# Feed-forward rows in tiles of 512 columns, and every product operand at 0 modulo 256 bytes

## The chip, the cores and the metric

The kernel runs on one core of one Trainium2 chip, as one launch. The metric is the device time of that launch in microseconds. Three runs before the change took 887.83 us in the median, from 887.15 to 888.42.

## The reference

The reference is one block of a hybrid network on 16 learned rows followed by 512 input rows, each of 1024 numbers in fp32:

```python
u = rms_norm(h, norm_mix_pre) @ w_in            # 528 x 1024 @ 1024 x (3*512 + 1792 + 2*1024)
u_sb, u_rw, gate_sb, gate_rw = split(u)
o_sb = stick_breaking_attention(*split(u_sb))   # 8 heads of 64
o_rw = rwkv7_time_mix(token_shift(u_rw), ...)   # 8 heads of 64, a recurrence over the rows
merged = sigmoid(gate_sb) * (o_sb @ w_branch_sb) + sigmoid(gate_rw) * (o_rw @ w_branch_rw)
h = h + rms_norm(merged @ w_out, norm_mix_post)
f = rms_norm(h, norm_ffn_pre)
f = (silu(f @ w_ffn_gate) * (f @ w_ffn_up)) @ w_ffn_down   # inner width 2816
h = h + rms_norm(f, norm_ffn_post)
return h[:, 16:]
```

## The kernel before

Activations lie transposed: features on the 128 partitions, rows of the sequence along the free axis. A matrix product is made on TensorE in the type fp32r, and for precision each operand is kept as a rounded half (`_hi`) and the rest (`_lo`). Three products stand for one: hi by hi, hi by lo, lo by hi. So each tile of 128 input features (`k`, eight of them for a width of 1024) costs three matmuls for each 128 output features, each matmul with its own weight load before it.

A weight tile is called a unit: 128 by 1024 numbers, 512 KB. SP loads it into one of four buffers `w_raw`, ScalarE rounds it to `w_hi` (two buffers), VectorE subtracts to `w_lo` (two buffers), and TensorE then makes 24 matmuls of it in `products` (L578 to L589). The units come in a fixed order, and semaphores count them: `w_split` after the subtraction, `w_used` after the last matmul.

The stages, in the order of time, and which operand streams through the array (moving) and which is loaded into it (stationary):

- The input projection (L586, in `products`) and ten of its gate units, which are cut in two halves and put between the steps of the mixing (L1672). Moving: `h_hi`, `h_lo`, the normed rows, 528 columns wide for each `k`. Stationary: `w_hi`, `w_lo`.
- The mixing of the heads, about 184 to 396 us: small fp32 matmuls of 64 by 64 (L1616), attention products (L1783 to L1847), and running sums with a triangle (L1818, L1824, L1828), where `softplus_hi` and `softplus_lo` are moving and `tri_r` is stationary. Each engine follows an order that is written out by hand.
- The branch products (L586 again, with `osb_hi`, `osb_lo`, `orw_hi`, `orw_lo` as the moving operand), with the same loop and the same order hi-hi, hi-lo, lo-hi.
- The output projection, in blocks of 128 rows (L1893, `block_products`): here the weights `wo_hi`, `wo_lo` (and `w_hi`, `w_lo`) are moving, in halves of 512 columns, and `merged_hi`, `merged_lo` are stationary. After each block VectorE and ScalarE norm the rows, TensorE transposes them (L1498), ScalarE copies the transposed block from PSUM into `h_hi` (L799, called by `out_hi`) and VectorE writes the rest into `h_lo` (L1112, called by `out_lo`). These are the feed-forward rows: 512 of them, written over the rows of the input projection, which is done by then.
- The first two feed-forward units (L1936) on the first 384 columns, with the last block's transposition between them, then on the last 128 columns.
- The other 42 feed-forward units (L586), a loop of four units a turn, moving `h_hi` and `h_lo`, 512 columns.
- The down projection (L1893): moving `w_hi`, `w_lo`, `wd_hi`, `wd_lo`, stationary `act_hi`, `act_lo`; and the last norm, of which little is left after the last product.

All of SBUF is laid out by hand with a running cursor (`sb`, L257), from the first byte that is free, 16,481 in this build, rounded up to 32: 16,512, which is 128 modulo 256. `h_hi` and `h_lo` are declared as [128, 8, 528] of four bytes, so that one `k` follows the other at 2,112 bytes, eight times 256 and 64. The weight buffers step by 512 bytes a `k`; `osb`, `orw`, `merged`, `act` by 2,048. The vector `p_chunk` (144 bytes) leaves the cursor 32 bytes off, so that `bonus` and all that lies behind it stand at 96 modulo 256.

Of the kernel before, what the change touches and what calls it, by code (L numbers as in the profile page):

```python
# [28 lines left out]
F32 = mybir.dt.float32  # L29
F32R = mybir.dt.float32r  # L30
# [4 lines left out]
P = 128  # L35
D = 1024
SEQ = 512
META = 16
T = META + SEQ
HALF = T // 2  # L40
KT = D // P
# [29 lines left out]

RAW = 4
SPL = 2

BLOCKS = (4, 0, 1, 2, 3)

# [52 lines left out]
OUT_ORDER = (0, 1, 2, 3)  # L129
FIRST = 3 * P  # L130
WO_FIRST = 2
OUT_BANKS = (6, 0, 2, 4)
# [114 lines left out]
def build(nc, x, meta, w_in, w_sb, w_rw, w_out, w_g, w_u, w_d, decay_up, aaa_up, gate_up,  # L247
          vecs, g_mix_pre, g_mix_post, g_ffn_pre, g_ffn_post, kf, kb, out):
    with ExitStack() as ctx:
# [5 lines left out]
        cursor = [base]  # L255

        def sb(name, shape, dt=F32):  # L257

            size = 1
            for n in shape[1:]:  # L260
                size *= n
            size *= 1 if dt == U8 else 4
            t = nc.alloc_sbuf_tensor_at(name, shape, dt, offset=cursor[0])
            cursor[0] += (size + 31) // 32 * 32
            assert cursor[0] <= end, (name, cursor[0], end)
            return t


        raw = [sb(f"w_raw{i}", [P, 1024]) for i in range(RAW)]
        w_hi, w_lo = [], []  # L270
        for i in range(SPL):
# [22 lines left out]
        h_hi = sb("h_hi", [P, KT, T], F32R)  # L294
        h_lo = sb("h_lo", [P, KT, T], F32R)
        ffn_at = cursor[0]
        cursor[0] = ffn_at - 2 * KT * T * 4
        held_hi = [sb(f"wd_hi{i}", [P, 1024], F32R) for i in range(HELD - SPL)]
        held_lo = [sb(f"wd_lo{i}", [P, 1024], F32R) for i in range(HELD - SPL)]
# [4 lines left out]
        kv_at = cursor[0]  # L304
# [9 lines left out]
        vv = sb("v_t", [P, PAIRS, TP])  # L314
        sg = sb("sig_xg", [P, T])
        pc = sb("p_chunk", [P, PAIRS, NC_])
        bonus_at = cursor[0]
        bonus = sb("bonus", [P, PAIRS, SEQ])
        mix_at = cursor[0]
# [111 lines left out]
        def bank(b, n=512):  # L431
            return psum[:, b, 0:n]
# [15 lines left out]
        def quads(b, n):  # L448

            return psum[:, b, 0:PAIRS * n].rearrange("p (q n) -> p q n", q=PAIRS)  # L450
# [12 lines left out]
        w_used = sem("w_used")  # L463
# [6 lines left out]
        n_lo = sem("norm_lo")  # L470
# [107 lines left out]
        def products(u, w0, outs, xh, xl, kts, last=False):  # L578

            hi, lo = w_hi[u % SPL], w_lo[u % SPL]  # L580
            n = 0
            total = 3 * len(kts)
            for i, k in enumerate(kts):
                for w, xs in ((hi, xh), (hi, xl), (lo, xh)):
                    for o, (c0, c1) in outs:
                        mm = nc.tensor.matmul(o, w[:, (w0 + i) * P:(w0 + i + 1) * P], xs[:, k, c0:c1],  # L586
                                              start=(n == 0), stop=(n == total - 1))
                    n += 1
            return mm  # L589
# [201 lines left out]
        def _(act):  # L791
            s_ = nc.scalar

            def norm_hi(n, width, c0, b=None):

                b = 4 + n % 4 if b is None else b
                for h in range(2):
                    act.wait_ge(n_tp, n + h + 1)
                    s_.activation(h_hi[:, 4 * h:4 * h + 4, c0:c0 + width], quads(b + h, width),  # L799
                                  ACT.Copy).then_inc(n_hi, 1)  # L800


# [109 lines left out]
            for kind, n, s in ORDER_ACT:  # L912
# [10 lines left out]
                if kind == "seq":  # L923
                    if s in ("bh", "kh"):
                        act.wait_ge(mix_pe, last_of(MIX_PE, "seq", c, ("T0", "T1", "T2")))
                        dst, c0 = {"bh": (bh, 0), "kh": (kh, 128)}[s]
# [22 lines left out]
                if kind == "sum":  # L949
# [9 lines left out]
                    if s == "w1":  # L959
                        act.wait_ge(mix_dve, last_of(MIX_DVE, "sum", h, ("s2", "s3")))  # L960
                        w = z_h[:, PART[1]]
                        s_.activation(w, w, ACT.Exp).then_inc(mix_act, 1)
                    if s == "w0":
                        act.wait_ge(mix_dve, last_of(MIX_DVE, "sum", h, ("s0", "s1")))
                        w = z_h[:, PART[0]]
                        s_.activation(w, w, ACT.Exp).then_inc(mix_act, 1)
                if kind == "att":
# [5 lines left out]
                    if s == "wm":  # L973
                        for h in (2 * n, 2 * n + 1):
                            act.wait_ge(mix_dve, upto(MIX_DVE, "sum", h, "s4"))
                        w = zm[n // 2][64 * (n % 2):64 * (n % 2) + 64, :]
# [6 lines left out]
            for kind, i in LATE:  # L983
# [20 lines left out]
                if kind == "unit":  # L1004
                    u = U_MIX + EARLY + i
# [52 lines left out]
                tail_root(b, TAIL_1_ACT.index(f"sq_f{n}") + 1)  # L1058

            def out_hi(n):  # L1060
                norm_hi(10 + 2 * n, P, P * OUT_ORDER[n], OUT_BANKS[OUT_ORDER[n]])

            out_square(0)
            out_square(1)
# [40 lines left out]
        def _(dve):  # L1105
            v_ = nc.vector

            def norm_lo(n, width, c0, b=None):
                b = 4 + n % 4 if b is None else b
                for h in range(2):  # L1110
                    dve.wait_ge(n_hi, n + h + 1)
                    v_.tensor_sub(h_lo[:, 4 * h:4 * h + 4, c0:c0 + width], quads(b + h, width),  # L1112
                                  h_hi[:, 4 * h:4 * h + 4, c0:c0 + width].bitcast(F32)).then_inc(n_lo, 1)

            def mean(i):

# [304 lines left out]
                v_.tensor_scalar(ztok[b][:], ztok[b][:], small[:, 24 + b:25 + b], None, ALU.mult).then_inc(tail_dve, 1)  # L1421

            def out_lo(n):
                norm_lo(10 + 2 * n, P, P * OUT_ORDER[n], OUT_BANKS[OUT_ORDER[n]])

            dve.wait_ge(rows_in, 48)
            out_gain(0)
# [60 lines left out]
        def _(pe):  # L1488
# [442 lines left out]
            def ffn_part(s, ks, c0, c1):  # L1931

                hi, lo = split(U_FFN + s)
                for k in ks:
                    for i, (w, xs) in enumerate(((hi, h_hi), (hi, h_lo), (lo, h_hi))):
                        mm = t_.matmul(psum[:, s, c0:c1], w[:, k * P:k * P + P], xs[:, k, c0:c1],  # L1936
                                       start=(k == 0 and i == 0), stop=(k == KT - 1 and i == 2))
                return mm
# [11 lines left out]
            def ffn_unit(i, s):  # L1950

                per = 2 * len(TAIL_FFN)
                ahead, t = s // RAW, s % RAW // 2
                u = U_FFN + s
                pe.wait_ge(w_split, i * RAW + (u + 1))
                step = 1 + s % 2
                pe.wait_ge(tail_dve, i * per + (FFN_AT + ahead * per + (t - 2) * len(TAIL_FFN) + step))
                products(u, 0, [(bank(s % RAW), (0, SEQ))], h_hi, h_lo, range(KT)).then_inc(w_used, 1)

            with pe.Fori(0, N_FFN_LOOP - 1) as i:  # L1960
                for s in range(2, RAW + 2):
# [72 lines left out]
```

## Time and profile before

| | |
|---|---|
| median of three runs | 887.83 us |
| span of the profiled execution | 883.6 us |
| left around the span | 4.2 us |
| TensorE | 98% of the span, 8165 matmuls |
| weight loads | 81%, beside the matmuls |
| VectorE, ScalarE, GpSimd | 55%, 47%, 11% |
| DMA | 82.82 MB, mean 94 GB/s |

The profiled execution's own time on the metric's clock is not given; the page has its span, from the first to the last instruction, and 4.2 us is the difference of that span to the median of the other three. A matmul's duration in the profile is modelled and longer than the time it holds the array, since the next one starts before the last has ended: the time that one costs is read from start to start.

### The profile page before, as it was taken

The numbers are of one execution on the slowest core, as the hardware profiler recorded it, in microseconds if no ns is written. First come the engines' busy times: TensorE is split into PE (matmuls) and PEld (weight loads), VectorE is DVE, ScalarE is ACT, GpSimd is POOL, SyncE is SP. The second block draws the span as 40 slices with busy tenths as digits, with TensorE's granted clock in tenths as the row PEclk, the third lists the DMA queues.
The fourth block names the chain that finished last, engine by engine and source line by source line (L and its number), as shares of the span: only waits on it lengthen the run. The fifth ranks groups of instructions, "written<-read, shape, count | busy, mean of one in ns | idle before, by whom it ended". The sixth has DMA issues, their size and how long they took to land.

```text
span 883.6 us, 18916 instructions
## 1 busy us (share of the span) xinstructions
PE 868.9 (98%) x8165; PEld 717.8 (81%) x8165; DVE 486.9 (55%) x642; ACT 411.2 (47%) x572; POOL 94.8 (11%) x92
## 2 busy tenths in 40 slices
PE   6999999999999999999999999999999999999997
PEld 5999999877877788668888898888888888888886
DVE  6459997245865767439575854444444444322333
ACT  6445566269777787464353532222222222211331
POOL 2015544111010111052000000000000000000000
PEclk9999999999999999999999999999999999999999
DMA  9332213321210011222369123333333333223321
GB/s 281 99 96 73 87 57 96 125 63 55 68 45 22 22 39 56 76 77 72 123 210 294 49 85 94 93 93 92 94 92 93 91 94 96 94 97 103 102 77 72
DMA packets 109584, 82.82 MB, mean 94 GB/s; under 512 B 3471, under 2 KB 100025, under 8 KB 109258
## 3 DMA queue, kind: packets, MB, share of 16 engines
q1 hardware_dynamic: 109514, 81.77, 30.4%
q8 instruction: 58, 0.95, 0.4%
q14 instruction: 12, 0.10, 0.0%
HBM read 75.99 MB, written 5.77 MB: 93 GB/s over the span
## 4 chain that ended last, share of the span: by engine, by line
PE 93%; DVE 4%; issue 1%; ACT 1%; DMA 0%; DVEq 0%; SPq 0%
PE psum L586 47%; PE psum L1893 19%; PE psum L1616 8%; PE psum L1672 7%; PE psum L1818 2%; PE psum L1936 2%; PE psum L1507 1%; PE psum L1828 1%; PE psum L1799 1%; DVE w_lo L576 1%; PE psum L1847 1%; DVE shift_diff L1178 1%; PE psum L1498 1%; DVE k_mod L1219 1%; DVE v_t L1183 1%
## 5 line engine op out<-in xcount | busy, mean ns | idle before, releaser
L586 PE MATMUL psum<-h_hi,w_hi 128*128 128x512 f32 (+2 forms) x736 | 230.2, 348 | 0.8 <-DVE w_lo L576 0.8
L586 PE MATMUL psum<-h_lo,w_hi 128*128 128x512 f32 (+2 forms) x736 | 229.4, 347 | 0.0
L586 PE MATMUL psum<-h_hi,w_lo 128*128 128x512 f32 (+2 forms) x736 | 228.5, 346 | 0.0
L576 DVE TENSOR_TENSOR w_lo<-w_raw,w_hi 128x1024 fp32r<-128x1024 f32 x69 | 88.8, 1288 | 120.9 <-ACT w_hi L571 116.5
L586 PEld LDWEIGHTS psum<-h_hi,w_hi 128*128 128x128 f32 x736 | 127.8, 188 | 22.3 <-issue 1.9
L586 PEld LDWEIGHTS psum<-h_lo,w_hi 128*128 128x128 f32 x736 | 127.5, 188 | 18.4 <-issue 0.5
L586 PEld LDWEIGHTS psum<-h_hi,w_lo 128*128 128x128 f32 x736 | 128.0, 188 | 17.8
L1090 ACT ACTIVATE w_hi<-w_raw 128x1024 fp32r<-128x1024 f32 x44 | 46.7, 1061 | 171.7 <-PE psum L586 164.4
L1453 DVE TENSOR_TENSOR w_lo<-w_raw,w_hi 128x1024 fp32r<-128x1024 f32 x44 | 53.9, 1225 | 130.6 <-ACT w_hi L1090 126.5
L571 ACT ACTIVATE w_hi<-w_raw 128x1024 fp32r<-128x1024 f32 x70 | 73.7, 1055 | 74.4 <-PE psum L1893 56.2
L1893 PE MATMUL psum<-w_hi,act_hi 128*128 128x512 f32 x144 | 45.7, 390 | 0.0
L1893 PE MATMUL psum<-w_hi,act_lo 128*128 128x512 f32 x144 | 45.7, 389 | 0.0
L1893 PE MATMUL psum<-w_lo,act_hi 128*128 128x512 f32 x144 | 45.7, 389 | 0.0
L1672 PE MATMUL psum<-h_hi,w_hi 128*128 128x512 f32 x80 | 32.7, 408 | 0.0
L1672 PE MATMUL psum<-h_lo,w_hi 128*128 128x512 f32 x80 | 31.7, 396 | 0.0
L1893 PEld LDWEIGHTS psum<-w_hi,act_hi 128*128 128x128 f32 x144 | 26.9, 188 | 5.8 <-DVE w_lo L576 0.2
L1893 PEld LDWEIGHTS psum<-w_hi,act_lo 128*128 128x128 f32 x144 | 27.0, 188 | 5.7
L1893 PEld LDWEIGHTS psum<-w_lo,act_hi 128*128 128x128 f32 x144 | 27.0, 188 | 5.6
L1672 PE MATMUL psum<-h_hi,w_lo 128*128 128x512 f32 x80 | 31.4, 393 | 0.0
L857 ACT ACTIVATE shift_in<-psum 128x528 f32<-128x528 f32 x14 | 8.6, 613 | 33.5 <-PE psum L586 29.8
L1336 DVE TENSOR_TENSOR scores<-scores,psum 128x128 f32<-128x128 f32 (+3 forms) x32 | 15.4, 482 | 13.1 <-PE psum L1828 12.7
L958 ACT ACT_TABLE_LOAD x16 | 20.5, 1283 | 0.3
(306 smaller groups left out, 1522.9 us busy)
## 6 DMA issues: line engine op xcount, KB each, us to landing
w_raw<-in_w_in SPq DMA_DIRECT2D x30, 512.0 KB, 3.8
w_raw<-in_w_g SPq DMA_DIRECT2D x22, 512.0 KB, 3.7
w_raw<-in_w_u SPq DMA_DIRECT2D x22, 512.0 KB, 3.8
w_raw<-in_w_d SPq DMA_DIRECT2D x22, 512.0 KB, 3.5
w_raw<-in_w_in SPq DMA_DIRECT2D x48, 128.0 KB, 2.2
w_raw<-in_w_out SPq DMA_DIRECT2D x8, 512.0 KB, 5.4
kept_gates<-gate_raw SPq DMA_DIRECT2D x10, 256.0 KB, 2.1
sig_t<-kept_gates SPq DMA_DIRECT2D x10, 256.0 KB, 2.8
```

Source lines behind the costliest of these rows:

```text
L571: nc.scalar.activation(split(u)[0][:], raw[u % RAW][:], ACT.Copy).then_inc(w_hi_done, 1)
L576: nc.vector.tensor_sub(lo[:], raw[u % RAW][:], hi[:].bitcast(F32)).then_inc(w_split, 1)
L586: mm = nc.tensor.matmul(o, w[:, (w0 + i) * P:(w0 + i + 1) * P], xs[:, k, c0:c1], start=(n == 0), stop=(n == total - 1))
L958: s_.activation(part, part, ACT.Ln, bias=1.0).then_inc(mix_act, 1)
L1090: s_.activation(w_hi[v % SPL][:], raw[v % RAW][:], ACT.Copy).then_inc(w_hi_done, 1)
L1336: v_.tensor_tensor(d, d, psum[:, CBANK, SEQ - WIDTH[j]:SEQ], ALU.subtract).then_inc(mix_dve, 1)
L1453: v_.tensor_sub(w_lo[v % SPL][:], raw[v % RAW][:], w_hi[v % SPL][:].bitcast(F32)).then_inc(w_split, 1)
L1616: mm = t_.matmul(psum[rows(p, hd, moved), bnk + p // 2, o0:o0 + n], w(k, p), m(k, p), start=first, stop=last, skip_group_check=True)
L1672: mm = t_.matmul(bank(GBANK), w[:, k * P:(k + 1) * P], xs[:, k, META:T], start=(k == 0 and i == 0), stop=(k == KT - 1 and i == 2))
L1818: t_.matmul(psum[:, CBANK, SEQ - WIDTH[i]:SEQ], tri_r[:, P:2 * P], part[:, OFF[i]:OFF[i] + WIDTH[i]], start=False, stop=False, skip_group_ ...
L1893: mm = t_.matmul(bank((2 * b if at is None else at) + h), xs[:, k, P * b:P * b + P], w[:, 512 * h:512 * h + 512], start=(k == 0 and i == 0 ...
L1936: mm = t_.matmul(psum[:, s, c0:c1], w[:, k * P:k * P + P], xs[:, k, c0:c1], start=(k == 0 and i == 0), stop=(k == KT - 1 and i == 2))
```

## The change

Five things are done.

1. Before the first buffer the cursor is rounded up to 256, so that memory begins at 16,640 and not at 16,512. Everything up to `p_chunk` moves by 128 bytes.
2. Before `bonus` the cursor is rounded up to the same place modulo 256 as `kT`, which moves `bonus` and all behind it by 160 bytes in all.
3. Two new tensors, `f_hi` and `f_lo`, are [128, 8, 512], one `k` every 2,048 bytes. They begin where `h_hi` and `h_lo` begin.
4. ScalarE and VectorE write the feed-forward rows into them.
5. All feed-forward products read them.

No instruction is added, removed or moved, and no wait is changed. `h_hi` and `h_lo` keep their 528 columns for the input projection and the gates.

```diff
+LINE = 256
@@ layout
+        cursor[0] += -cursor[0] % LINE
         raw = [sb(f"w_raw{i}", [P, 1024]) for i in range(RAW)]
...
         ffn_at = cursor[0]
+        f_hi, f_lo = (nc.alloc_sbuf_tensor_at(n, [P, KT, SEQ], F32R, offset=ffn_at - i * KT * T * 4)
+                      for n, i in (("f_hi", 2), ("f_lo", 1)))
...
         pc = sb("p_chunk", [P, PAIRS, NC_])
+        cursor[0] += (kv_at - cursor[0]) % LINE
         bonus_at = cursor[0]
@@ ScalarE
-            def norm_hi(n, width, c0, b=None):
+            def norm_hi(n, width, c0, b=None, hi=h_hi):
...
-                    s_.activation(h_hi[:, 4 * h:4 * h + 4, c0:c0 + width], quads(b + h, width),
+                    s_.activation(hi[:, 4 * h:4 * h + 4, c0:c0 + width], quads(b + h, width),
...
             def out_hi(n):
-                norm_hi(10 + 2 * n, P, P * OUT_ORDER[n], OUT_BANKS[OUT_ORDER[n]])
+                norm_hi(10 + 2 * n, P, P * OUT_ORDER[n], OUT_BANKS[OUT_ORDER[n]], f_hi)
@@ VectorE
-                    v_.tensor_sub(h_lo[:, 4 * h:4 * h + 4, c0:c0 + width], quads(b + h, width),
-                                  h_hi[:, 4 * h:4 * h + 4, c0:c0 + width].bitcast(F32)).then_inc(n_lo, 1)
+                    v_.tensor_sub(lo[:, 4 * h:4 * h + 4, c0:c0 + width], quads(b + h, width),
+                                  hi[:, 4 * h:4 * h + 4, c0:c0 + width].bitcast(F32)).then_inc(n_lo, 1)
@@ TensorE, ffn_part
-                    for i, (w, xs) in enumerate(((hi, h_hi), (hi, h_lo), (lo, h_hi))):
+                    for i, (w, xs) in enumerate(((hi, f_hi), (hi, f_lo), (lo, f_hi))):
@@ TensorE, ffn_unit
-                products(u, 0, [(bank(s % RAW), (0, SEQ))], h_hi, h_lo, range(KT)).then_inc(w_used, 1)
+                products(u, 0, [(bank(s % RAW), (0, SEQ))], f_hi, f_lo, range(KT)).then_inc(w_used, 1)
```

Where the operands of the fp32r products stand, modulo 256 bytes, worked out from the layout code:

| stage | moving before | stationary before | moving after | stationary after |
|---|---|---|---|---|
| input projection, gates | 128 + 64k, plus 64 or 32 by column | 128 | 64k, plus the same | 0 |
| running sums | 96 | 128 | 0 | 0 |
| branches | 128 | 128 | 0 | 0 |
| output projection | 128 | 96 | 0 | 0 |
| feed-forward | 128 + 64k | 128 | 0 | 0 |
| down projection | 128 | 128 | 0 | 0 |

## Rows read from the trace of the kernel before

**Rows 1.** Page, part 2, granted TensorE clock in 40 slices, tenths

```profile
PEclk9999999999999999999999999999999999999999
```

**Rows 2.** Chain that ended last, in time: start, length (us), what, count

```profile
387.38 1.72 PE psum L1860 x4
...
396.40 65.99 PE psum L586 x288
462.38 33.59 PE psum L1893 x144
...
497.72 8.40 PE psum L1893 x36
507.00 2.79 PE psum L1893 x12
509.79 6.86 PE psum L1936 x39
...
519.10 5.57 PE psum L1936 x48
524.67 233.66 PE psum L586 x1008
758.33 119.90 PE psum L1893 x528
```

**Rows 3.** Timeline of TensorE, feed-forward: start, modelled duration (us), every third matmul

```profile
599.71 0.39 PE L586 MATMUL psum<-h_hi,w_hi 128*128 128x512 f32 x1
...
600.40 0.40 PE L586 MATMUL psum<-h_hi,w_hi 128*128 128x512 f32 x1
...
601.10 0.40 PE L586 MATMUL psum<-h_hi,w_hi 128*128 128x512 f32 x1
...
601.79 0.39 PE L586 MATMUL psum<-h_hi,w_hi 128*128 128x512 f32 x1
...
602.49 0.39 PE L586 MATMUL psum<-h_hi,w_hi 128*128 128x512 f32 x1
```

**Rows 4.** Timeline of TensorE, branch products: first and last of 57 in a row

```profile
424.82 0.39 PE L586 MATMUL psum<-osb_hi,w_hi 128*128 128x512 f32 x1
...
437.51 0.39 PE L586 MATMUL psum<-osb_hi,w_lo 128*128 128x512 f32 x1
```

**Rows 5.** Timeline, all engines, around the last block's transposition

```profile
514.83 0.75 DVE L1421 TENSOR_SCALAR z_tok<-z_tok,small 128x1024 f32<-128x1024 f32 x1
...
516.49 1.03 PE L1498 MATMUL psum<-consts,z_tok 128*128 128x128 f32 x8
517.12 1.09 ACT L799 ACTIVATE h_hi<-psum 128x512 fp32r<-128x512 f32 x2 [2.52 <-PE psum L1498]
...
517.75 1.29 DVE L1112 TENSOR_TENSOR h_lo<-psum,h_hi 128x512 fp32r<-128x512 f32 x2 [2.17 <-ACT h_hi L799]
...
519.10 0.33 PE L1936 MATMUL psum<-h_hi,w_hi 128*128 128x128 f32 x1
```

**Rows 6.** Groups by line, 530 to 750 us: busy, mean ns, idle before, releaser

```profile
L1453 DVE TENSOR_TENSOR w_lo<-w_raw,w_hi 128x1024 fp32r<-128x1024 f32 x40 | 49.0, 1225 | 119.0 <-ACT w_hi L1090 119.0
L1090 ACT ACTIVATE w_hi<-w_raw 128x1024 fp32r<-128x1024 f32 x40 | 42.4, 1061 | 156.0 <-PE psum L586 156.0
```

**Rows 7.** Groups by line and shape, TensorE, whole span: busy, mean ns, idle

```profile
L1616 PE MATMUL psum<-consts,x_inv 64*64 64x64 f32 x704 | 15.2, 219 | 0.0
...
L1824 PE MATMUL psum<-meta_softplus_lo,tri_r 128*128 128x512 f32 x8 | 3.2, 394 | 0.0
```

**Rows 8.** Timeline of TensorE, small products of the mixing: two groups and their successors

```profile
184.20 0.69 PE L1616 MATMUL psum<-a_r,b_t 64*64 64x64 f32 x32
184.72 0.30 PE L1616 MATMUL psum<-b_t,a_r 64*64 64x64 f32 x8
...
197.19 0.65 PE L1616 MATMUL psum<-consts,x_inv 64*64 64x64 f32 x32
197.66 0.24 PE L1616 MATMUL psum<-v_tm,aak 64*64 64x64 f32 x4
```

More of the change, by code:

```diff
@@ L1106, in _, with norm_lo @@
             v_ = nc.vector
-            def norm_lo(n, width, c0, b=None):
+            def norm_lo(n, width, c0, b=None, hi=h_hi, lo=h_lo):
                 b = 4 + n % 4 if b is None else b
@@ L1423, in out_lo @@
             def out_lo(n):
-                norm_lo(10 + 2 * n, P, P * OUT_ORDER[n], OUT_BANKS[OUT_ORDER[n]])
+                norm_lo(10 + 2 * n, P, P * OUT_ORDER[n], OUT_BANKS[OUT_ORDER[n]], f_hi, f_lo)
             dve.wait_ge(rows_in, 48)
```

## The prediction

> **What bounds the kernel now.** I read the chain of work that ended last first, since it says which engine the end hangs on: after 396 us it is made of long pieces of TensorE matmuls and almost nothing else, 233.66 us of feed-forward products and 119.90 us of the down projection among them [rows 2]. TensorE's clock is granted in full throughout [rows 1], which is the upper of its two levels, 2.4 GHz, so nothing is to be had there. The groups by line show the other side: in 220 us of feed-forward the two engines that prepare weights sit idle for 156.0 us waiting for TensorE and 119.0 us for one another [rows 6]. So the kernel is bound by how fast TensorE takes one matmul after another, and the only question is what a matmul costs from start to start.
>
> Then the same thing by stage. 512 columns at 2.4 GHz are 213.3 ns. Feed-forward: 233.66 us / 1008 = 231.8 ns. Four of its tiles, twelve matmuls, take 602.49 - 599.71 = 2.78 us, 231.7 ns each, and the four triples 0.69, 0.70, 0.69 and 0.70 us [rows 3]. Branches: (437.51 - 424.82) us / 56 = 226.6 ns [rows 4]. Down: 119.90 / 528 = 227.1, its tail included. Output projection: 33.59 / 144 = 233.3 [rows 2]. The branches and the feed-forward are the same line with the same three products in the same order, each matmul with a weight load of 128 columns before it. What differs is where the operands lie. The branches and the down projection, with both operands at 128 modulo 256, run at 226.6 to 227.1; the output projection, 128 against 96, and the feed-forward, whose tiles step by 64 so that one in four agrees with its weights, run at 231.8 to 233.3. I read from this that two streams, the moving operand and the next weights, are taken at full rate only when they stand at the same place modulo 256.
>
> **The change, part by part.** No instruction and no wait is added, so the sum is one of rates. I take 226.7 ns as the target, between rows 4 and the down projection.
>
> Feed-forward loop: after the change tile and weights agree in every k. 1008 x (231.8 - 226.7) = 5.1 us. The ends: nothing, if the distance of `h_lo` from `h_hi` (16,896 bytes, kept by `f_lo` and `f_hi`) is what costs and not the step of a tile; and 1008 x (231.8 - 215) = 16.9 us if 0 is better than 128, where 215 is the fastest stream of 512 columns in the trace, the fp32 products of L1860, which take 1.72 us / 4 = 430 ns for an instruction that the clock lets stream its columns twice [rows 2]. I take the branches' row as the nearest: same line, same loop, tiles at a step of 2,048 bytes.
>
> The Trainium skill says in "TensorE: Matmul & The Clock Gate" (what happens when you issue a matmul, step 1) that TensorE reads moving data and weights through two independent ports, so that loading the next weights takes nothing from a running matmul. By it addresses are no matter and the sum would be 0. This trace disagrees, with 231.8 against 226.6 ns on one line.
>
> First two units: the 39 matmuls of 384 columns before the last transposition take 6.86 us, 175.9 ns each [rows 2]; at the aligned rate per column, 226.7 / 512 x 384 = 170.0, they give 0.2 us. The nine after it give nothing: TensorE begins the last 128 columns at 519.10, just as VectorE ends the last `h_lo` at 517.75 + 1.29 = 519.04 [rows 5], so that chain, from the transposes on, sets the time. The transposes themselves are not held up: their rows are ready at 514.83 + 0.75 = 515.58, 0.9 us before 516.49 [rows 5], and 0.2 us is gained there. The 48 matmuls of 128 columns stand at 5.57 / 48 = 116 ns [rows 2], where their columns alone would take a quarter of 226.7, 57 ns. The ends are nothing and 48 x 59 = 2.8 us. The eight transposes, as narrow, take 1.03 / 8 = 129 ns with both operands as they were [rows 5], so width is not what limits a narrow one; I take 0.1 us, near the lower end.
>
> Output projection: 144 + 36 + 12 matmuls in 33.59 + 8.40 + 2.79 = 44.78 us are 233.2 ns each [rows 2]; 192 x (233.2 - 226.7) = 1.2 us. Ends: nothing and 192 x 18.2 = 3.5 us.
>
> Running sums: `softplus` goes from 96 to 0 and the triangle from 128 to 0. Their 512-column rows have a modelled duration of 394 ns [rows 7], where the branches have 0.39 us and the feed-forward 0.39 to 0.40 [rows 3, 4], so they are no better than mixed. 144 such matmuls of all widths at 5.1 ns at most are 0.7 us; the mixing is not TensorE's alone, so I take 0.3.
>
> Small products of the mixing: 704 of them read `x_inv` (96 before) against `consts` (128) and agree afterwards [rows 7]. The trace has 32 such in 0.47 us, 14.7 ns each, and 32 with both at 128 in 0.52 us, 16.3 ns [rows 8]. If that were the address, agreement would cost 704 x 1.6 = 1.1 us; if it went the other way, as in the wide ones, it would give as much. The difference is as easily the groups' own, so I take 0 and keep 1.1 on both sides.
>
> Input projection and gates: both operands move by 128 together, the step of 2,112 stays: 0. Branches and down projection: likewise, from 128 and 128 to 0 and 0: 0, on the ground that only the difference counts; the rivals price the doubt. The writes of `f_hi` and `f_lo` are the same instructions with another step of k; 0, and what hides a few ns of them is rows 5's slack for all blocks but the last, where they would be on the path (four instructions).
>
> What is late next in the feed-forward: a unit goes from 24 x 231.8 = 5.56 us to 5.44. ScalarE's rounding, 1.06 us, and VectorE's subtraction, 1.23, begin when TensorE lets go of the buffer and have one whole unit's time for 2.3 us of work [rows 6]; no wait comes up.
>
> Sum: 5.1 + 0.2 + 0.1 + 1.2 + 0.3 = 6.9 us. The span goes from 883.6 to 876.7, and with the 4.2 us around it the time from 887.8 to **880.9 us**.
>
> **The rivals.**
>
> *It is not the address modulo 256.* If the distance of the two halves or the like sets the feed-forward's rate, `f_hi` and `f_lo` change nothing in 1008 matmuls, and only the output projection, 1.2 us, and the sums may gain: 886.5 us. For it: the triple in which tile and weights both stand at 128 takes 0.69 us and not the branches' 0.68 [rows 3]; the feed-forward's four triples differ by less than they all do from the branches. Against it: the output projection has a third distance and is slow too. The skill's rule of the two ports gives about this time as well.
>
> *0 is better than 128.* Then all 1920 aligned matmuls gain: 16.9 us in the feed-forward, 192 x 18.2 = 3.5 in the output projection, and (192 + 528) x (227 - 215) = 8.6 in branches and down projection, 29 us: 859 us. For it: an aligned matmul still stands 13 ns above its columns' time while an fp32 one stands 2 above. Against it: the tile that stands at 0, between two at 192 and 64, has no cheaper triple, though its weights stood at 128. The skill (same page, "Back-to-back issue gap") has N/2.4 + 2.5 ns for a warm matmul, 215.8 for 512 columns; no fp32r row here shows it.
>
> *Slower: 128 is what counts.* If the fast rate belongs to 128 itself (both operands in the second half of a 256-byte line) and 0 and 0 run as mixed ones do, the down projection and the branches lose (528 + 192) x (231.8 - 226.7) = 3.7 us, the feed-forward stays, and the output projection gains 192 x 1.4 = 0.3: 891.2 us. It decides as soon as the 720 lose more than the 1008 gain. For it: no pair at 0 and 0 exists in the trace. Against it: the fast stages have nothing else in common than that their operands agree, and no row ties the rate to 128 itself.
>
> **How the numbers follow.** The forecast 0.62, its own range 878.5 to 883.5 (sums and small products by 1.1 each way, the target between 226 and 228). Not the address: 0.14. Better at 0: 0.12. Slower: 0.08. Something between the first two, such as a feed-forward at 229: 0.04. What a measurement of this kernel can tell from no change is about 0.2%, 1.8 us. Faster is forecast, better at 0 and the one between, 0.78; same 0.14; slower 0.08. The range 873 to 888 takes in the forecast, the one between and the first rival, and leaves out 0.2.
>
> **What would show it.** The piece of 1008 feed-forward matmuls should take 228.5 us, with all triples at 0.68; 144 of the output projection 32.6; the 528 of the down projection 119.9 as before. The third rival would show in that last number, at 122.6, the second at 114 or less. Wrong would be: a feed-forward piece over 232, a down projection changed by over 1 us, or a mixing that ends elsewhere against its start by over 1 us.

## The result: 879.99 us, 0.992 of the time before

Five runs of the changed kernel took 879.99 us in the median (879.50 to 881.18), five of the kernel before beside them 887.15 us. The ratio is 0.9919, with a 95% interval from 0.9907 to 0.9931, so 7.2 us were saved, 6.1 to 8.3. The forecast was 880.9 us, with 878.5 to 883.5 as its own range, and 6.9 us saved.

The profiled execution has a span of 878.0 us and a time of 879.9 us. So 1.9 us lie around the span, not the 4.2 us that I had taken from the kernel before. That difference compared the span of one execution with the median of others, and executions of one kernel are some 2 us apart (last section). The span that I had forecast, 876.7 us, is 1.3 us under the measured one; the forecast time is nearer than its own working.

The chain that ended last, in order of time (start, length in us, what, how many), of the changed kernel. Its lines stand 6 lower in the file: L592 is L586 of before, L1899 is L1893.

```profile
397.01 65.96 PE psum L592 x288
462.97 32.72 PE psum L1899 x144
...
497.44 8.19 PE psum L1899 x36
506.51 2.73 PE psum L1899 x12
509.25 6.79 PE psum L1942 x39
516.90 7.15 PE psum L1942 x57
524.05 228.66 PE psum L592 x1008
752.71 119.88 PE psum L1899 x528
```

Beside [rows 2]: the 1008 feed-forward matmuls went from 233.66 to 228.66 us, which is 5.0 us or 231.8 to 226.8 ns each. The 192 of the output projection went from 44.78 to 32.72 + 8.19 + 2.73 = 43.64 us, 1.1 us less. The down projection stayed, 119.90 and 119.88. The first units (39 matmuls) gave 0.07 us. That is 6.2 us. What lies before 397 us has to be looked at on its own, since this execution reaches the first of these pieces 0.6 us later than before.

TensorE's timeline in the feed-forward, the first and the last of thirteen in a row, in the stretch of [rows 3]: start, modelled duration.

```profile
599.78 0.39 PE L592 MATMUL psum<-f_lo,w_hi 128*128 128x512 f32 x1
...
602.50 0.39 PE L592 MATMUL psum<-f_lo,w_hi 128*128 128x512 f32 x1
```

Twelve matmuls in 2.72 us, where [rows 3] have 2.78.

The 0.6 us is one stop, which the timeline of TensorE shows in the middle of 32 like matmuls, and for which no semaphore is named:

```profile
313.15 0.40 PE L1622 MATMUL psum<-w_inv,xt 64*64 64x64 f32 x13
313.96 0.56 PE L1622 MATMUL psum<-w_inv,xt 64*64 64x64 f32 x19 [0.41 <-issue]
```

The same program's next profile has it at the same instruction, half as long:

```profile
315.07 0.40 PE L1622 MATMUL psum<-w_inv,xt 64*64 64x64 f32 x13
315.69 0.56 PE L1622 MATMUL psum<-w_inv,xt 64*64 64x64 f32 x19 [0.21 <-issue]
```

Its length changes from execution to execution of one program, so I don't count it to the change. Of the fourteen profiles of this case, seven have it at this instruction, 0.21 to 0.67 us long, among them the kernel before with nothing but its memory moved by 128 bytes (base only, below); the kernel before has none there, but neither have two kernels below whose memory begins where the changed kernel's does (`f_lo` alone moved; halves apart). So the place of the memory alone doesn't decide it, and what it is stays open.

### The profile page after: what moved, and what is told of

It reads as the page before. It is cut to its first block, busy times and chain, and to the rows that moved or that the text cites. A ratio compares the mean times of both kernels' runs of the same rounds, so it can differ in the third digit from the quotient of the medians.

```text
span 878.0 us, 18916 instructions
## 1 busy us (share of the span) xinstructions
PE 862.6 (98%) x8165; PEld 717.7 (82%) x8165; DVE 487.1 (55%) x642; ACT 411.1 (47%) x572; POOL 94.1 (11%) x92
## 4 chain that ended last, share of the span: by engine, by line
PE 93%; DVE 4%; issue 1%; ACT 1%; DMA 0%; DVEq 0%; SPq 0%
PE psum L592 47%; PE psum L1899 19%; PE psum L1622 8%; PE psum L1678 7%; PE psum L1824 2%; PE psum L1942 2%; PE psum L1513 1%; PE psum L1834 1%; PE psum L1805 1%; DVE w_lo L582 1%; PE psum L1853 1%; DVE shift_diff L1184 1%; PE psum L1504 1%; DVE k_mod L1225 1%; DVE v_t L1189 1%
## 5 line engine op out<-in xcount | busy, mean ns | idle before, releaser
L592 PE MATMUL psum<-f_hi,w_hi 128*128 128x512 f32 x336 | 130.8, 389 | 0.0
L592 PE MATMUL psum<-f_lo,w_hi 128*128 128x512 f32 x336 | 130.7, 389 | 0.0
L592 PE MATMUL psum<-f_hi,w_lo 128*128 128x512 f32 x336 | 130.7, 389 | 0.0
L1096 ACT ACTIVATE w_hi<-w_raw 128x1024 fp32r<-128x1024 f32 x44 | 46.7, 1061 | 166.7 <-PE psum L592 159.4
L1459 DVE TENSOR_TENSOR w_lo<-w_raw,w_hi 128x1024 fp32r<-128x1024 f32 x44 | 53.9, 1226 | 125.6 <-ACT w_hi L1096 121.4
L592 PE MATMUL psum<-h_hi,w_hi 128*128 128x264 f32 (+2 forms) x400 | 98.2, 310 | 0.8 <-DVE w_lo L582 0.8
L592 PE MATMUL psum<-h_lo,w_hi 128*128 128x264 f32 (+2 forms) x400 | 96.5, 306 | 0.0
L592 PE MATMUL psum<-h_hi,w_lo 128*128 128x264 f32 (+2 forms) x400 | 96.5, 306 | 0.0
L592 PEld LDWEIGHTS psum<-f_hi,w_hi 128*128 128x128 f32 x336 | 63.1, 188 | 13.2
L592 PEld LDWEIGHTS psum<-f_hi,w_lo 128*128 128x128 f32 x336 | 63.1, 188 | 13.1
L592 PEld LDWEIGHTS psum<-f_lo,w_hi 128*128 128x128 f32 x336 | 63.1, 188 | 13.0
L592 PEld LDWEIGHTS psum<-h_hi,w_hi 128*128 128x128 f32 x400 | 64.7, 188 | 7.1 <-issue 1.9
L592 PEld LDWEIGHTS psum<-h_lo,w_hi 128*128 128x128 f32 x400 | 64.5, 188 | 3.8 <-issue 0.5
L592 PEld LDWEIGHTS psum<-h_hi,w_lo 128*128 128x128 f32 x400 | 64.8, 188 | 3.4
L1899 PE MATMUL psum<-w_hi,act_hi 128*128 128x512 f32 x144 | 45.7, 390 | 0.0
L1899 PE MATMUL psum<-w_lo,act_hi 128*128 128x512 f32 x144 | 45.7, 389 | 0.0
L1899 PE MATMUL psum<-w_hi,act_lo 128*128 128x512 f32 x144 | 45.7, 389 | 0.0
L1899 PEld LDWEIGHTS psum<-w_hi,act_lo 128*128 128x128 f32 x144 | 27.0, 188 | 5.7
L1899 PEld LDWEIGHTS psum<-w_lo,act_hi 128*128 128x128 f32 x144 | 27.0, 188 | 5.7
```

The source lines that it names most:

```text
L1096: s_.activation(w_hi[v % SPL][:], raw[v % RAW][:], ACT.Copy).then_inc(w_hi_done, 1)
L1459: v_.tensor_sub(w_lo[v % SPL][:], raw[v % RAW][:], w_hi[v % SPL][:].bitcast(F32)).then_inc(w_split, 1)
L1899: mm = t_.matmul(bank((2 * b if at is None else at) + h), xs[:, k, P * b:P * b + P], w[:, 512 * h:512 * h + 512], start=(k == 0 and i == 0 ...
```

## The experiments

All ratios are to the kernel before, run beside them. "Difference" is the moving operand's place less the stationary one's, modulo 256 bytes.

**The changed kernel again.** No edit.

> The changed kernel once more, beside the three below. Ratio to before 0.992. In its profile the 1008 feed-forward matmuls take 228.7 us, the 144 of the output projection 32.7, the 528 of the down projection 119.9. The first look at the changed kernel had TensorE stand still for 0.4 us at 313.5 us, with no semaphore behind it. If that was chance it is gone or elsewhere, and the feed-forward begins 1.2 us earlier than before the change; if the moved memory causes it, it is there again at the same place and the feed-forward begins 0.6 us earlier.

881.02 us, ratio 0.9928 (0.9916 to 0.9941). Feed-forward 228.64 us, output projection 32.72, down 119.85. The stop is there again, at the same instruction, at 0.21 us. The feed-forward begins 1.1 us later than before the change, and not 0.6 us earlier: this execution lost 2.0 us at its start (last section). From the last units of the input projection to the branches it takes 230.4 us, where the kernel before took 230.0, so nothing is gained before 396 us.

**Tiles only.** The two roundings of the cursor are taken out, `f_hi` and `f_lo` stay:

```diff
-        cursor[0] += -cursor[0] % LINE
-        cursor[0] += (kv_at - cursor[0]) % LINE
```

> Only the feed-forward tiles are packed at 2,048 bytes a k; memory begins at 16,512 as before and bonus stays at 96. If what counts is that moving and stationary operand agree modulo 256: feed-forward piece 228.6 us (both at 128), output projection still 33.6, down 119.9, running sums as before, time 5.1 us under before (ratio 0.9943). If 0 counted: the feed-forward stays at 233.7 and the ratio is 1.000.

881.67 us, ratio 0.9943 (0.9931 to 0.9955), as the agreement of places has it. The chain:

```profile
462.78 33.60 PE psum L1897 x144
...
525.00 228.66 PE psum L590 x1008
753.66 119.82 PE psum L1897 x528
```

The feed-forward has the whole gain with both operands at 128; the output projection, whose `merged` is still at 96, has none.

**Base only.** The kernel before with the first rounding alone.

```diff
+        cursor[0] += -cursor[0] % LINE
         raw = [sb(f"w_raw{i}", [P, 1024]) for i in range(RAW)]
```

> Only the first rounding up of the cursor, on the kernel before: all operands move by 128, nothing else agrees or disagrees with anything that it did not before (tile step 2,112, merged 32 off). If only agreement counts: no change, ratio 1.000 within 0.002, feed-forward 233.7, output projection 33.6, down 119.9. If 128 were the good place, down and branches would lose 3.7 us; if 0 were, they would gain.

887.32 us, ratio 1.0001 (0.9993 to 1.0010). The chain:

```profile
464.69 33.58 PE psum L1896 x144
...
526.97 233.66 PE psum L589 x1008
760.62 119.81 PE psum L1896 x528
```

Down and branches run at 0 as they ran at 128: 119.81 us against 119.90, and 66.03 against 65.99 for the piece of 288 matmuls that holds the branches. Moving the whole memory is worth nothing.

**Everything at 128.** The whole change without its first rounding:

```diff
-        cursor[0] += -cursor[0] % LINE
```

> The whole change but for the first rounding up: every aligned operand stands at 128 and not at 0. If only agreement counts: the same time as the changed kernel, ratio to before 0.992, feed-forward 228.6, output projection 32.7. If 0 is worth something of its own, this one is slower than the changed kernel, by up to the whole 7 us.

881.65 us, ratio 0.9935 (0.9923 to 0.9947), which overlaps both measurements of the changed kernel. The pieces are those of the changed kernel to 0.04 us:

```profile
465.44 32.71 PE psum L1898 x144
...
526.50 228.65 PE psum L591 x1008
755.15 119.84 PE psum L1898 x528
```

So two of the three rivals are out: 0 is not better than 128, and 128 is not better than 0.

That the places must agree modulo 256 bytes and not modulo 512 or more, the layout shows: before the change `osb_hi` and `osb_lo` stood 256 bytes from their weights modulo 512 and `orw_hi` and `orw_lo` 0, and both ran at the rate of [rows 4], whose 57 matmuls hold both; after it, the feed-forward's tiles stand 256 from theirs modulo 512.

**Out of agreement again, a constant a stage.** Three kernels put each stage's operand by a constant; the first of them:

```diff
-        f_hi, f_lo = (nc.alloc_sbuf_tensor_at(n, [P, KT, SEQ], F32R, offset=ffn_at - i * KT * T * 4)
-                      for n, i in (("f_hi", 2), ("f_lo", 1)))
+        f_hi, f_lo = (nc.alloc_sbuf_tensor_at(n, [P, KT, SEQ], F32R, offset=ffn_at - i * KT * T * 4 + d)
+                      for n, i, d in (("f_hi", 2, 64), ("f_lo", 1, 64)))
...
-        cursor[0] = kv_at
+        cursor[0] = kv_at + 32
         osb_hi = sb("osb_hi", [P, PAIRS, SEQ], F32R)
...
-        cursor[0] = bk_at
+        cursor[0] = bk_at + 32
...
-        act_hi = at(act_at, "act_hi", [P, FT, SEQ], F32R)
+        act_hi = at(act_at + 32, "act_hi", [P, FT, SEQ], F32R)
```

> The changed kernel with its operands put out of agreement again, each stage by one constant: feed-forward tiles 64 bytes after their weights (moving minus stationary = 64), branches 32, down projection -32 (act 32 after). If only exact agreement modulo 256 is fast and every other difference costs alike: feed-forward 233 ns a matmul (235 us), branches and down 233 ns (down 123 us). If the cost grows with the distance: 32 is cheaper than 64, some 228 and 230 ns. If a granule of 64 bytes is what matters and not 256, the feed-forward stays at 226.8 and the two others rise.

In the second the same lines have 128 for the tiles of the feed-forward, 64 for `osb` and `orw`, 128 for `act_hi`, and `merged` is put 128 further; in the third `f_hi` stays at 0 and `f_lo` has 64, `osb` and `orw` have 128, `act_hi` 64.

> As before this one, other constants: feed-forward 128, branches 64, output projection (merged 128 after) -128, down projection (act 128 after) -128. All or nothing: 233 ns in each of the four. Growing with distance: 128 is the dearest, some 235 ns, branches less. Granule of 64 or 128 bytes: all stay at 226.8.

> f_hi stays with its weights and f_lo alone is 64 bytes off: one matmul in three of the feed-forward disagrees; branches 128, down projection -64. If each matmul pays for its own disagreement: the feed-forward's mean is a third of the way from 226.8 to what 64 costs in the feed-forward of the first of these kernels. If a disagreement is carried into the matmuls after it (before the change the triple in which all stood at 128, between others that did not, cost 691 and not 680 ns), the mean lies further up, towards the whole.

The three ran once each, 887.66, 890.38 and 889.83 us, beside one run of the kernel before at 885.73. One run can't tell a microsecond, but its pieces can be compared: the 144 of the output projection, which the first and the third leave alone, take 32.72 us in both, as in the changed kernel.

Chains of the three: the piece of 288 (96 gates and 192 branch products), in the second the output projection, the feed-forward, and the down projection:

```profile
397.89 67.22 PE psum L592 x288
...
526.19 230.87 PE psum L592 x1008
757.06 123.20 PE psum L1899 x528
```

```profile
397.20 66.39 PE psum L592 x288
463.59 33.59 PE psum L1899 x144
...
525.85 234.38 PE psum L592 x1008
760.23 122.74 PE psum L1899 x528
```

```profile
396.99 67.03 PE psum L592 x288
...
525.12 233.99 PE psum L592 x1008
759.11 123.21 PE psum L1899 x528
```

Divided by the counts (for the branches: 226.7 and the difference to the changed kernel's 65.96 us, over 192):

| difference, constant | ns a matmul of 512 columns | stage |
|---|---|---|
| 0 | 226.8, 227.0, 227.2 | feed-forward, down, output projection |
| +32 | 233.3 | branches; output projection before |
| -32 | 233.3 | down |
| +64 | 229.0 | feed-forward, branches |
| -64 | 233.4 | down |
| 128 | 232.5, 232.3, 233.3, 232.5 | feed-forward, branches, output projection, down |
| 0, +64, 0 by turns (f_lo alone moved) | 232.1 | feed-forward |

None of the three expectations for constant differences holds as written. It is not all or nothing, since +64 costs only 2.2 ns; it does not grow with distance, since 32 costs more than 64; and no granule of 64 or 128 is free. The last line is the telling one: if each matmul paid for its own difference, two at 226.8 and one at 229.0 would be 227.5. It is 232.1, dearer than either, and beyond the range that the expectation of the third kernel gave for a disagreement that is carried on. It matters, then, where the operand of the matmul before stood.

**Input projection, halves apart.** From here on the aim is the stages that still step by 64 a k.

```diff
-            n = 0
...
-            for i, k in enumerate(kts):
-                for w, xs in ((hi, xh), (hi, xl), (lo, xh)):
-                    for o, (c0, c1) in outs:
+            for o, (c0, c1) in outs:
+                n = 0
+                for i, k in enumerate(kts):
+                    for w, xs in ((hi, xh), (hi, xl), (lo, xh)):
...
```

> The changed kernel, with one order changed: in the input projection a unit's first 264 columns are done for all k, then its last 264, where the two alternated before (they stand 32 bytes apart modulo 256). Same instructions, same weights, tiles still step by 64 against their weights. If changing the difference from one matmul to the next is what costs, the 264-column matmuls fall from 121.9 ns by 1 or 2 ns, up to 1.9 us in all, ratio 0.990; if only the sum of single differences counts, nothing changes: 0.992.

880.06 us, ratio 0.9920 (0.9907 to 0.9933): nothing. The 264-column matmuls stand at 121.8 ns from start to start, in the mean, against 121.9. The step of the tiles is still there.

**Weights that step along.** `w_hi` and `w_lo` of the input projection and gates get 576 bytes a k, so that tile and weights agree, or differ by one constant, in every k. The columns' halves are apart as in the run above, the memory's start is not rounded, so constants stand at 128 as in everything at 128, and `sa_st`, which has no room left, goes elsewhere:

```diff
+WP = 144
-            w_hi.append(sb(f"w_hi{i}", [P, 1024], F32R))
+            w_hi.append(sb(f"w_hi{i}", [P, KT * WP], F32R))
+        def spread(w):
+            return w[:, 0:KT * WP].rearrange("p (k n) -> p k n", k=KT)[:, :, 0:P]
...
-            nc.scalar.activation(split(u)[0][:], raw[u % RAW][:], ACT.Copy).then_inc(w_hi_done, 1)
+            dst = spread(split(u)[0]) if apart(u) else split(u)[0][:, 0:1024]
+            src = raw3(u) if apart(u) else raw[u % RAW][:]
+            nc.scalar.activation(dst, src, ACT.Copy).then_inc(w_hi_done, 1)
...
+            step = WP if apart(u) else P
...
-                        mm = nc.tensor.matmul(o, w[:, (w0 + i) * P:(w0 + i + 1) * P], xs[:, k, c0:c1],
+                        mm = nc.tensor.matmul(o, w[:, (w0 + i) * step:(w0 + i) * step + P], xs[:, k, c0:c1],
```

> Weights of the input projection and gates are written with 576 bytes from one k to the next instead of 512, so that they step along with the tiles of 2,112 (all memory 128 lower and one small buffer elsewhere to make room), and halves are done apart. The difference is then constant: 0 for first halves, 32 for last, 64 for gates. By the rates found (226.7, 233.3, 229.0 ns a 512 columns): 264 columns at 117 and 120.4 ns, gates 229.0. 944 x 3.2 + 442 x 3.0 = 4.4 us under the changed kernel, ratio to before 0.987. If a constant difference is worth nothing here (the writes of ScalarE and VectorE slower, or weights at another step collide), the ratio stays 0.992 or is above it.

The second: weights of gates and q start 16 numbers further in, where the tile's columns start that they meet.

```diff
+        def skip(u):
+            return META if u >= U_MIX or ORDER[u][0] == "sq" else 0
...
-            return w[:, 0:KT * WP].rearrange("p (k n) -> p k n", k=KT)[:, :, 0:P]
+            return w[:, 0:KT * WP].rearrange("p (k n) -> p k n", k=KT)[:, :, skip(u):skip(u) + P]
...
-                        mm = t_.matmul(bank(GBANK), w[:, k * WP:k * WP + P], xs[:, k, META:T],
+                        mm = t_.matmul(bank(GBANK), w[:, k * WP + META:k * WP + META + P], xs[:, k, META:T],
```

> The one before, and gate and q weights also start 64 bytes further in, so that they agree with rows that begin at column 16: difference 0 for them. Gates from 229.0 to 226.7: 442 x 2.3 = 1.0 us more, ratio 0.986. This is the version that the rates point to.

The third: the first, with the halves of the columns by turns again, as in the changed kernel.

```diff
-            for o, (c0, c1) in outs:
-                n = 0
-                for i, k in enumerate(kts):
-                    for w, xs in ((hi, xh), (hi, xl), (lo, xh)):
+            n = 0
+            for i, k in enumerate(kts):
+                for w, xs in ((hi, xh), (hi, xl), (lo, xh)):
+                    for o, (c0, c1) in outs:
...
```

> The spread weights with first and last halves alternating again: the difference goes 0, 32, 0, 32 from matmul to matmul. If each matmul pays its own difference: 118.7 ns in the mean, as with halves apart. If a change of difference costs of its own, more than 118.7, up to the 121.9 of before.

879.32 us and 0.9911 (0.9896 to 0.9925); 880.25 us and 0.9922 (0.9907 to 0.9937); 880.59 us in the one run of the third. The forecasts of 0.987 and 0.986 fell. The gates of the second, whose tile and weights stand at the same place in every k, in TensorE's timeline, twelve matmuls:

```profile
409.61 0.40 PE L611 MATMUL psum<-h_hi,w_hi 128*128 128x512 f32 x1
...
412.39 0.40 PE L611 MATMUL psum<-h_hi,w_hi 128*128 128x512 f32 x1
```

2.78 us, 231.7 ns each, to the hundredth what the feed-forward took before the change, although here no matmul's two operands disagree. Agreement alone is not enough. The first of the three is half a microsecond better in the input projection (the 72 matmuls of its last q units take 16.82 us against 16.90) but not told apart from the changed kernel by its time. None of them is a version that beats it.

Agreement does not even come first here. The 96 gates before the branches, in the first:

```profile
396.55 22.15 PE psum L607 x96
```

That is 230.7 ns each at a difference of 64 in every k. Start to start, the same gates take 232.4 ns in the changed kernel, 230.7 in the third and 231.6 in the second, whose operands agree. The 264-column matmuls go from 121.9 to between 121.4 and 121.6 ns in the three, half a nanosecond of the 3.2 that were forecast, and the third, which alternates between two differences, is not dearer than the first.

**All at 64, one tile moved.** Two things can explain that: these tiles pass through places 64 and 192, or they step.

```diff
         cursor[0] += -cursor[0] % LINE
+        cursor[0] += 64
...
-        o_at = [ffn_at + n for n in (26880, 35072, 61696, 69888, 0, 45312)]
+        o_at = [ffn_at + n for n in (26880, 35072 + 64, 61696, 69888, 0, 45312)]
...
-        cursor[0] = kv_at
+        cursor[0] = kv_at + 96
...
-        cursor[0] = bk_at
+        cursor[0] = bk_at + 96
```

> Why did the spread weights not help, though tile and weights agreed in every k? Theory A, the step: a matmul is only fast if its operands stand where those of the one before stood, modulo 256; a tile step of 2,112 moves both by 64 every third matmul. Theory B, the place: 0 and 128 are good places and 64 and 192 are not, and the spread tiles passed through all four. Here the whole memory of the changed kernel stands at 64, all agreeing, steps unchanged: A has the feed-forward at 228.6 us and the down projection at 119.9, B has them at 233 to 235 and 122.7. In the output projection one of the eight weight tiles (k = 3) stands 64 bytes further: if each matmul pays only its own difference (229.0 ns at +64), the 24 of it cost 0.06 us more; if the step costs of its own, up to 0.2 us more. The branches stand at +96, a difference not yet measured: 226.7 to 233.3.

One run, 882.39 us, beside one of the kernel before at 888.11. The chain:

```profile
465.33 32.92 PE psum L1900 x144
...
500.00 8.27 PE psum L1900 x36
...
526.69 228.66 PE psum L593 x1008
755.35 119.84 PE psum L1900 x528
```

At 64, with everything constant, feed-forward and down are as fast as at 0 and 128, so of theory B nothing is left but the place 192, which no run tried by itself. (The branches, at +96, take 233.2 ns.) The one moved tile speaks for the step. It costs 0.20 us in 144 matmuls, three blocks of rows with six matmuls each that differ by 64, which by the constant rate would be 18 x 2.2 ns = 0.04; the fourth block adds 0.08 (8.27 against 8.19 us). Where the 0.2 us sits can be seen in the timeline behind the moved tile, two matmuls a row, all of them in agreement again:

```profile
476.19 0.63 PE L1900 MATMUL psum<-wo_hi,merged_hi 128*128 128x512 f32 x2
...
478.51 0.62 PE L1900 MATMUL psum<-wo_hi,merged_lo 128*128 128x512 f32 x2
...
483.05 0.61 PE L1900 MATMUL psum<-wo_hi,merged_hi 128*128 128x512 f32 x2
```

The first ten take 2.32 us, 232 ns each; the next twenty 4.54 us, 227 ns. After a step it takes some ten matmuls until the fast rate is back, though nothing stands at another place than 64 in them. The changed kernel shows the same without any step, behind a wait of 40 ns for a weight tile (the pair at 465.53 is that much longer):

```profile
465.53 0.67 PE L1899 MATMUL psum<-w_hi,merged_hi 128*128 128x512 f32 x2
466.03 0.62 PE L1899 MATMUL psum<-w_lo,merged_hi 128*128 128x512 f32 x2
...
467.88 0.62 PE L1899 MATMUL psum<-w_hi,merged_lo 128*128 128x512 f32 x2
...
468.78 0.61 PE L1899 MATMUL psum<-wo_lo,merged_hi 128*128 128x512 f32 x2
```

From 466.03 to 467.88 four pairs take 1.85 us, 231 ns a matmul; from 467.88 to 468.78 two take 0.90, 225 to 227. At the feed-forward's start six matmuls are enough. So two streams, moving data and the next weights, come into a fast rhythm only after six to ten matmuls in which their places agree and stay. A tile step of 2,112 bytes breaks it every third matmul and it is never reached; that is the reading of [rows 2, 3] that fits all runs. It is shown by the moved tile and by the tiles alone; for the spread weights it is argued, since no run took the step away from them. What in the memory makes the rhythm was not seen, nor why +64 costs less than the other differences.

## Why the prediction was right, and where not

- **What bounds the kernel**: right. TensorE's rate alone moved the time, and in the feed-forward loop no other wait came up. What [rows 6] showed is the same in the changed kernel's page, which is over the whole span: ScalarE's `w_hi` of L1096 waits for TensorE for most of its idle time, VectorE for ScalarE.

```profile
L1096 ACT ACTIVATE w_hi<-w_raw 128x1024 fp32r<-128x1024 f32 x44 | 46.7, 1061 | 166.7 <-PE psum L592 159.4
L1459 DVE TENSOR_TENSOR w_lo<-w_raw,w_hi 128x1024 fp32r<-128x1024 f32 x44 | 53.9, 1226 | 125.6 <-ACT w_hi L1096 121.4
```

- **Feed-forward**, 5.1 us forecast: 5.0. **Output projection**, 1.2: 1.1. **Down, branches, input projection**, 0: 0. The loop at 226.8 ns is the branches' row carried over, and that it carried is what made the number.
- **First units**, 0.2 us before the transposes: 0.07. The term was mis-sized by its rate. I scaled 226.7 ns by the columns, to 170.0 for 384; in agreement they take 6.79 us / 39 = 174.1. What stands over the columns' own time is 13.5 ns at 512 columns and 14.1 at 384: it is nearer an amount a matmul than a share. The 48 of 128 columns, 0.1: nothing (57 matmuls, nine of them wide, in 7.15 us, before 1.57 and 5.57). The 129 ns that I set beside them for the transposes is their modelled duration over eight; from their start to the next matmul's, at 517.28 us, they took 0.79 us, 99 ns each.
- **The last columns wait for VectorE** [rows 5]: right, and the wait that was just under way has now opened. `f_lo` ends at 517.13 + 1.29 = 518.42, TensorE goes on at 518.48, and its weight load has sat idle for it:

```profile
517.13 1.29 DVE L1118 TENSOR_TENSOR f_lo<-psum,f_hi 128x512 fp32r<-128x512 f32 x2 [2.10 <-ACT f_hi L805]
...
518.48 0.19 PEld L1942 LDWEIGHTS psum<-f_hi,w_hi 128*128 128x128 f32 x1 [0.32 <-DVE f_lo L1118]
```

- **Running sums**, 0.3: nothing. Their 512-column rows, but for the first of each group, have modelled durations of 391 to 397 ns, as in [rows 7], and start to start, in the mean of all that have another such behind them, they take 258.9 ns, before 259.2. They come in twos and fours between other products, so a rhythm that takes six to ten matmuls is not reached; this is argued from the runs above, not tried. **Small products**, 0 within 1.1: 0, 15.2 us and 219 ns as in [rows 7]:

```profile
L1622 PE MATMUL psum<-consts,x_inv 64*64 64x64 f32 x704 | 15.2, 219 | 0.0
...
L1830 PE MATMUL psum<-meta_softplus_lo,tri_r 128*128 128x512 f32 x8 | 3.2, 396 | 0.0
```

- **Not the address** (first rival): wrong, by the tiles-only run; the distance of the halves is the same there and the gain is whole. But what I had noted for it, that the agreeing triple took 0.69 us and not 0.68, was the hint at the part of the mechanism that my reading lacked. The prediction said that the streams go at full rate "only when they stand at the same place"; the fuller rule is the same place, and the same as in the matmuls before. That the forecast did not hang on the difference was luck, as the packed tiles happen to bring both. The extension built on my half of the rule (weights that step along) did, and failed.
- **Better at 0** and **slower, 128 counts**: wrong, by base only and everything at 128.
- The Trainium skill's two independent ports ("TensorE: Matmul & The Clock Gate", what happens when you issue a matmul) would, if nothing else ties the two together, have made all these layouts alike; 226.8 to 233.4 ns by layout alone contradicts that reading. The 215.8 ns that the Trainium skill's formula gives for a warm matmul of 512 columns ("Back-to-back issue gap", same page) was reached by no fp32r matmul with a weight load before each in any run here.
- The sum of the pieces is 6.2 us, of the 6.9 forecast; the medians are 7.2 and, in the second measurement, 6.0 us apart. The intervals hold 6.2, so that 7.2 came out nearer to 6.9 than the pieces do is chance.

## What to carry to other kernels

Where a TensorE-bound loop runs full-width fp32r matmuls, let tile and weight strides be multiples of 256 bytes and let both operands start at the same place modulo 256; which place it is did not matter for the three that were tried (0, 64, 128), so padding the base buys nothing. Compare the start-to-start time of stages that run the same instruction on other buffers: a 2% difference between them is a layout that can be had for nothing. Test a rule on a second stage before building on it, since one that fits all rows may be half of it.

## What the runs showed of the hardware

- The streams' rhythm, for fp32r matmuls of 512 columns with a weight load before each: 226.8 ns in agreement, 229.0 to 233.4 at other constant differences, 230.7 to 232.4 where they step, and about ten matmuls to come back after a step or a wait of 40 ns.
- Executions of one program differ by 2 us, and a part of it is TensorE's clock at the start. In one of the changed kernel's two profiles the first projection matmuls of 264 columns start every 0.12 us, in the other every 0.22, which is their columns at the lower level, 1.2 GHz. In both, TensorE had run short transposes and then waited, 1.36 and 1.19 us. The trace's record of the granted clock has the upper level from 13.7 us after the span's start in the one and from 19.9 us in the other, and in all fourteen profiles it is so: seven have it from before 15 us and start these matmuls every 0.12 us, seven from 18.6 to 20.0 us and start them every 0.22. For the time before, the trace has no record, and the views print 1.00 there, [rows 1] too. Nor does the mean granted clock of the span show it, 1.000 and 0.998 for these two but 1.000 also for everything at 128, where these matmuls start every 0.22: what lowers the mean is the last 0.3 to 3.3 us of the span, at the lower level. What decides how early the upper level comes stays open. The first lines of that stretch in each:

```profile
15.62 0.29 PE L1513 MATMUL psum<-h_lo,w_hi 128*128 128x264 f32 x1
15.75 0.28 PE L1513 MATMUL psum<-h_hi,w_lo 128*128 128x264 f32 x1
```

```profile
15.84 0.42 PE L1513 MATMUL psum<-h_lo,w_hi 128*128 128x264 f32 x1
16.06 0.42 PE L1513 MATMUL psum<-h_hi,w_lo 128*128 128x264 f32 x1
```

By the sixteenth of these matmuls (at 18.12 us in the one, 20.20 in the other) this alone puts one execution 2.0 us behind the other, more than a quarter of what the change is worth. Spans of single profiles are to be compared by their pieces.
